# The first seven-product round's weight sums ahead of the low parts of x, and two of those low parts on GpSimd

## The reference

```python
def swiglu(x, w_gate, w_up, w_down):
    return (jax.nn.silu(x @ w_gate) * (x @ w_up)) @ w_down
f = swiglu(rms_norm_2(h, ffn1_pre_norm[l]), ffn1_w_gate[l], ffn1_w_up[l], ffn1_w_down[l])
h = h + FFN_RESIDUAL_WEIGHT * rms_norm_2(f, ffn1_post_norm[l])
```

## Time and profile before

| | us |
|---|---|
| median of three runs | 1831.26 |
| lowest, highest | 1829.66, 1832.38 |
| the profiled execution's own time | 1829.83 |
| its span in the trace | 1827.7 |
| TensorE busy | 1792.5 (98%) |
| GpSimd busy | 1286.9 (70%) |
| VectorE busy | 1126.0 (62%) |
| ScalarE busy | 710.5 (39%) |

### The profile page before, as it was taken

One profiled execution on the slowest core, in us unless ns is written; L12 is line 12 of the kernel. 1 busy time (PEld: TensorE's weight loads), 2 busy tenths in 40 slices (PEclk: granted clock), 3 DMA queues, 4 the chain that ended last, 5 costly groups with the idle time before them and its releaser, 6 DMA issues.

```text
span 1827.7 us, 28330 instructions
## 1 busy us (share of the span) xinstructions
PE 1792.5 (98%) x10236; PEld 1528.0 (84%) x10236; DVE 1126.0 (62%) x1741; ACT 710.5 (39%) x1337; POOL 1286.9 (70%) x1190
## 2 busy tenths in 40 slices
PE   9999999999999999999999999999999998999998
PEld 7888888878878899998888877798876778999886
DVE  5166774149984798887016767574454189888731
ACT  3111111127762366552014267553413255666001
POOL 7766666767777798877667865453772687888775
PEclk9999999999999999999999999999999999999999
DMA  5222223232223323235223311201321222323421
GB/s 187 94 91 92 92 92 138 92 120 78 89 69 116 131 100 103 106 109 189 95 92 104 103 60 47 69 26 47 116 95 44 93 110 76 115 96 113 165 101 69
DMA packets 25886, 179.36 MB, mean 98 GB/s; under 512 B 2864, under 2 KB 2992, under 8 KB 6704
## 3 DMA queue, kind: packets, MB, share of 16 engines
q1 hardware_dynamic: 24048, 168.31, 26.0%
q10 hardware_dynamic: 1728, 9.58, 1.4%
HBM read 171.58 MB, written 6.29 MB: 97 GB/s over the span
## 4 chain that ended last, share of the span: by engine, by line
PE 84%; DVE 8%; ACT 3%; issue 3%; POOL 1%; DMA 1%; DVEq 0%; ACTq 0%; POOLq 0%
PE bank L457 12%; PE bank L458 12%; PE bank L459 12%; PE bank L1216 6%; PE bank L1218 6%; PE bank L1217 6%; PE bank L1666 2%; PE bank L1667 2%; PE bank L1668 2%; PE bank L495 2%; PE bank L496 2%; PE bank L497 2%; DVE temps L1397 1%; PE bank L2071 1%; PE bank L2347 1%
## 5 line engine op out<-in xcount | busy, mean ns | idle before, releaser
L350 POOL TENSOR_TENSOR weights_lo<-raw_weights,weights_hi 128x512 fp32r<-128x512 f32 (+4 forms) x416 | 558.8, 1343 | 41.2 <-ACT weights_hi L369 7.4
L348 POOL TENSOR_SCALAR weights_hi<-raw_weights 128x512 fp32r<-128x512 f32 (+4 forms) x392 | 268.0, 684 | 340.1 <-PE bank L459 173.7
L457 PE MATMUL bank<-x_hi,weights_hi 128*128 128x512 f32 x688 | 271.5, 395 | 0.2
L459 PE MATMUL bank<-x_lo,weights_hi 128*128 128x512 f32 x688 | 267.9, 389 | 0.0
L458 PE MATMUL bank<-x_hi,weights_lo 128*128 128x512 f32 x688 | 267.8, 389 | 0.0
L457 PEld LDWEIGHTS bank<-x_hi,weights_hi 128*128 128x128 f32 x688 | 129.2, 188 | 28.1 <-POOL weights_lo L350 0.8
L459 PEld LDWEIGHTS bank<-x_lo,weights_hi 128*128 128x128 f32 x688 | 129.1, 188 | 27.1
L458 PEld LDWEIGHTS bank<-x_hi,weights_lo 128*128 128x128 f32 x688 | 129.2, 188 | 26.9 <-issue 1.0
L1218 PE MATMUL bank<-x_lo,weights_hi 128*128 128x256 f32 x432 | 122.2, 283 | 0.0
L1258 POOL TENSOR_TENSOR weights_lo<-temps,weights_hi 128x512 fp32r<-128x512 f32 x72 | 108.1, 1521 | 2.7 <-ACT weights_hi L1290 2.7
L1258 POOL TENSOR_TENSOR weights_lo<-raw_weights,weights_hi 128x512 fp32r<-128x512 f32 x72 | 97.6, 1360 | 13.3 <-ACT weights_hi L1290 13.0
(11 more groups left out here) (552 smaller groups left out, 5076.6 us busy)
## 6 DMA issues: line engine op xcount, KB each, us to landing
raw_weights<-in_ffn_seven SPq DMA_DIRECT2D x36, 1024.0 KB, 4.7
raw_weights<-in_a_ug SPq DMA_DIRECT2D x16, 1024.0 KB, 4.8
raw_weights<-in_b_in SPq DMA_DIRECT2D x12, 1024.0 KB, 4.8
raw_weights<-in_ffn_down SPq DMA_DIRECT2D x12, 1024.0 KB, 4.7
raw_weights<-in_ffn_down SPq DMA_DIRECT2D x7, 1408.0 KB, 6.2
raw_weights<-in_a_out SPq DMA_DIRECT2D x8, 1024.0 KB, 4.8
raw_weights<-in_ffn_up SPq DMA_DIRECT2D x8, 1024.0 KB, 4.8
raw_weights<-in_a_v SPq DMA_DIRECT2D x7, 1024.0 KB, 4.8
```

The lines of the kernel that those rows point to most:

```text
L348: nc.gpsimd.tensor_scalar(hi, raw, 1.0, 0.0, ALU.mult, ALU.add).then_inc(S("units_hi"), 1)
L350: nc.gpsimd.tensor_tensor(lo, raw, hi.bitcast(F32), ALU.subtract).then_inc(units_ready, 1)
L457: nc.tensor.matmul(ps, wh, xh[:, k, :], start=k == 0, stop=False)
L459: last = nc.tensor.matmul(ps, wh, xl[:, k, :], start=False, stop=k == last_k)
```

## The change

The four weight sums of round 0 and M5's low stand on VectorE behind plain round 1, ahead of the lows of x; the lows of x are then only numbers 0 and 1. Numbers 2 and 3 are made by GpSimd, behind its lows of M6 and M7 of round 0. So that the sums may lie in T[3] early, plain round 2 gates into T[1] instead of T[3], and ScalarE's copy of M5's half result (which also goes to T[1]) waits for that round's low. ScalarE makes the highs of M1, M5, M6, M3, M7 ahead of plain round 2's silu, M2's behind that round, and moves low 3 only behind M6's copy.

```diff
--- before.py
+++ after.py
@@ -169,7 +169,7 @@
     [("b_thr", KB), ("seven_hi", 2 * PRODUCTS * SEVEN)], [("b_a", KB), ("seven_kept", 2 * 3 * SEVEN)], [("b_scan", KB), ("seven_sums", 2 * 4 * SEVEN)],
     [("b_y", KB), ("seven_gates", 2 * SEVEN)], [("b_ix", KB), ("seven_joined", 2 * SEVEN)], [("b_bterm", KB), ("seven_lo_by_dve", 2 * SEVEN)],
     [("a_vn", KA), ("seven_lo", 2 * POOL_LOWS * SEVEN)], [("a_spatial", KA), ("seven_used", 2 * PRODUCTS * SEVEN)], [("b_tl", KB), ("kept_x", 5)],
-    *([(early, n)] + _members(kind, ("ffn1", each), ("ffn2", each)) for early, n, kind, each in (("b_a2", KB, "mixed_hi", 4), ("b_m2", KB, "mixed", 4), ("a_s_read", KA, "mixed_lo", 4), ("b_thi", KB, "moved", 2))),
+    *([(early, n)] + _members(kind, ("ffn1", each), ("ffn2", each)) for early, n, kind, each in (("b_a2", KB, "mixed_hi", 4), ("b_m2", KB, "mixed", 4), ("a_s_read", KA, "mixed_lo", 2), ("b_thi", KB, "moved", 2), ("a_gu", KA, "mixed_lo_by_pool", 2))),
     [("raw_first2", 16), ("spilled", 32)], [("raw_first3", 16), ("reloaded", 32)], [("x_in2", 16), ("raw_rest", 16)],
     [("b_mult", KB)] + _members("gained", ("ffn1", KD), ("ffn2", KD)),
     [("fx_o", FOXH), ("ma_o", 2 * MH)], [("fx_hi", FOXH // 2), ("ma_hi", 2 * MH)], [("fx_lo", FOXH // 2), ("ma_lo", 2 * MH)],
@@ -1225,10 +1225,10 @@
                     return lambda k: x[MIX_OF[p]][:, k, :]
 
                 def mixed_ready(t):
-                    if r == 0:
+                    if r == 0 and t < 2:
                         pe.wait_ge(*due(f"{f}_mixed_lo", t + 1))
-                        if t >= 2:
-                            pe.wait_ge(*due(f"{f}_moved", t - 1))
+                    elif r == 0:
+                        pe.wait_ge(*due(f"{f}_moved", t - 1))
 
                 pe_bank_read(pe, f, g, 1)
                 product(M1, up[:, A_HALF], plain(XH, 0, A_HALF), plain(XL, 0, A_HALF), True)
@@ -1248,6 +1248,10 @@
                 mixed_ready(3)
                 product(M4, up[:, A_HALF], mixed(MIX_H, M4), mixed(MIX_L, M4), False)
 
+        def pool_mixed_low(pool, f, t):
+            pool.wait_ge(*due(f"{f}_mixed_hi", t + 1))
+            nc.gpsimd.tensor_tensor(LOW_AT[t], MIX[t], MIX_H[t].bitcast(F32), ALU.subtract).then_inc(S(f"{f}_mixed_lo_by_pool"), 1)
+
         def pool_seven(pool, ph):
 
             for r in range(SEVEN):
@@ -1256,6 +1260,8 @@
                         continue
                     pool.wait_ge(*due("seven_hi", seven_count(ph, r, p)))
                     nc.gpsimd.tensor_tensor(RING_LO[p], source_of(r, p), RING_HI[p].bitcast(F32), ALU.subtract).then_inc(S("seven_lo"), 1)
+                    if r == 0 and p in (M6, M7):
+                        pool_mixed_low(pool, ph.name[:4], 2 if p == M6 else 3)
 
         def act_gained(act, f, src, gain, ready):
 
@@ -1273,7 +1279,7 @@
 
         def act_move_low(act, f, t):
             act.wait_ge(units_used, PH[f"{f}_up"].used(HEAD - 1, 3))
-            act.wait_ge(*due(f"{f}_mixed_lo", t + 1))
+            act.wait_ge(*due(f"{f}_mixed_lo_by_pool", t - 1))
             nc.scalar.activation(MIX_L[t], LOW_AT[t].bitcast(F32), ACT.Copy).then_inc(S(f"{f}_moved"), 1)
 
         def act_seven_hi(act, ph, r, p):
@@ -1305,16 +1311,16 @@
             ph = PH[f"{f}_seven"]
             for g in range(HEAD - 1):
                 if g == HEAD - 2:
-                    act_seven_hi(act, ph, 0, M1)
+                    for p in (M1, M5, M6, M3, M7):
+                        act_seven_hi(act, ph, 0, p)
                 act_silu(act, f, g, T[:, 0, :])
                 if f == "ffn2" and g == 0:
                     act_mixed_hi(act, f, 1)
                     act_mixed_hi(act, f, 2)
-                act_y_hi(act, f, g, T[:, 3, :])
+                act_y_hi(act, f, g, gated_tile(g))
                 if f == "ffn2" and g == 0:
                     act_mixed_hi(act, f, 3)
-            for p in range(M5, M4):
-                act_seven_hi(act, ph, 0, p)
+            act_seven_hi(act, ph, 0, M2)
             for r in range(SEVEN):
                 g, more = HEAD + r, r + 1 < SEVEN
                 gate, up = PS[2 * (r % 2)], PS[2 * (r % 2) + 1]
@@ -1324,14 +1330,17 @@
                 act_keep(act, ph, r, M1, KEPT[:, A_HALF], up[:, A_HALF])
                 if r == 0:
                     act_move_low(act, f, 2)
-                    act_move_low(act, f, 3)
                 if more:
                     act_seven_hi(act, ph, r + 1, M1)
+                if r == 0:
+                    act.wait_ge(*due(f"{f}_yl", HEAD - 1))
                 act_keep(act, ph, r, M5, KEPT5, gate[:, B_HALF])
                 if more:
                     act_seven_hi(act, ph, r + 1, M5)
                 act_y_hi(act, f, g - 1, old_up)
                 act_keep(act, ph, r, M6, KEPT[:, B_HALF], up[:, A_HALF])
+                if r == 0:
+                    act_move_low(act, f, 3)
                 if not more and f == "ffn1":
                     after_seven(act)
                 if more:
@@ -1346,6 +1355,10 @@
                 act_silu(act, f, g, T[:, 0, :])
                 act_y_hi(act, f, g, T[:, 3, :])
 
+        def gated_tile(g):
+
+            return T[:, 1 if g == HEAD - 2 else 3, :]
+
         def dve_ffn_plain(dve, f, ph, r, g, before_gated=None, before_low=None):
 
             bank = 2 * (g % 2)
@@ -1357,11 +1370,11 @@
                 before_gated()
             dve.wait_ge(*due(f"{f}_tu", g + 1))
             dve.wait_ge(*due(f"{f}_sg", g + 1))
-            nc.vector.tensor_tensor(T[:, 3, :], T[:, 1, :], T[:, 2, :], ALU.mult).then_inc(S(f"{f}_y"), 1)
+            nc.vector.tensor_tensor(gated_tile(g), T[:, 1, :], T[:, 2, :], ALU.mult).then_inc(S(f"{f}_y"), 1)
             if before_low:
                 before_low()
             dve.wait_ge(*due(f"{f}_yh", g + 1))
-            nc.vector.tensor_tensor(Y_L[:, g, :], T[:, 3, :], Y_H[:, g, :].bitcast(F32), ALU.subtract).then_inc(S(f"{f}_yl"), 1)
+            nc.vector.tensor_tensor(Y_L[:, g, :], gated_tile(g), Y_H[:, g, :].bitcast(F32), ALU.subtract).then_inc(S(f"{f}_yl"), 1)
 
         def dve_mix_x(dve, f, t):
 
@@ -1431,13 +1444,13 @@
             else:
                 dve_ffn_plain(dve, f, head, 0, 0)
             dve_ffn_plain(dve, f, head, 1, 1)
-            for t in range(4):
-                dve_mixed_low(dve, f, t)
-            dve_ffn_plain(dve, f, head, 2, 2)
-            dve.wait_ge(*due(f"{f}_yl", HEAD - 1))
+            dve.wait_ge(*due(f"{f}_yl", HEAD - 2))
             for p in (M5, M6, M3, M7):
                 dve_seven_sum(dve, ph, 0, p)
             dve_seven_low(dve, ph, 0)
+            for t in range(2):
+                dve_mixed_low(dve, f, t)
+            dve_ffn_plain(dve, f, head, 2, 2)
             last_head = HEAD - 1
             dve.wait_ge(units_used, head.used(last_head, 1))
             dve_gate_scaled(dve, f, PS[2 * (last_head % 2)])
```

## The result

The changed kernel has a median of 1833.6 us over 20 runs, the kernel before one of 1830.74 over 20 runs beside it: a ratio of 1.0015 with a 95% interval of 1.0008 to 1.0022. So it is slower, by 2.9 us, which is under the 0.2% that I had set as the bound of "no change" while the interval reaches over it. The span of the profiled execution went from 1827.7 to 1830.8 us.

A forecast was written before the change was run, and what follows sets the result against it. TensorE bounds the kernel, busy 1792.5 of 1827.7 us; M5's 3.3 us wait for VectorE's low was the longest. First FFN +3.1 and second +1.0 gave +4.1 on 1831.26, so 1835.4 us; range 1830.5 to 1838.0.

The forecast's parts named there:

- M1 waits in place of M5: Second FFN, first seven-product round: M1 waits for plain round 2's scalings to free its bank, starting 4.3 us late.
- A GpSimd low of x blocks for its whole length: VectorE beside GpSimd's 1024-wide lows: each low takes 2.4 us alone and holds VectorE up for all of it.
- The bound from a 512-wide block: Lower bound on VectorE's hold-up by a GpSimd low of x: 1.1 us, making the change's sum about zero (-0.2).
- The second FFN by round 3: Net delay of TensorE in the second FFN by round 3 of the seven-product rounds: +1.0 us.
- The first FFN: Gating and a sum fall behind GpSimd's wide lows, M4 in round 0 comes +2.9 us late; +3.1 by round 3.
- The turns of the later rounds: VectorE and GpSimd sharing time in the next two rounds: joins late by some tenths, as before.
- The total: Whole kernel: +3.1 in the first FFN and +1.0 in the second, together +4.1 us, so 1835.4.
- my likeliest class: Whole kernel's outcome: slower, chance 0.52, with the forecast just above the 0.2% (3.7 us) bound of no change.
- The named wait: Second FFN, before the change: M5's wait for its low on VectorE, with the slow clock behind it, costing about 4.8 us.
- the third rival: Both FFNs' pauses grow, a turn lost in each and the clock fallen in both: +6.9 us, 1838.2; chance 0.10.
- the simple replacement: M1 waits in M5's place, but wide GpSimd lows hold VectorE up little: -0.2 us, 1831.1; chance 0.22.
- The one in which GpSimd loses the turns: VectorE runs at its lone prices, M5's wait and slow clock go in the second FFN: -4.7 us, 1826.6; chance 0.10.

The follow-up runs named there:

- e3: The change with GpSimd's two wide lows shrunk to one column each, the low part of x in M7 and M4 not computed: 1827.74 us, ratio 0.9977 to before.
- v1: Kernel before with plain rounds 1 and 2 worked in banks and VectorE ordered by due dates, no low of x on GpSimd: 1827.0 us, ratio 0.9977.
- v2: Kernel before with VectorE ordered by due dates (M5's sum and low early), plain rounds not in banks: 1831.33 us, ratio 1.0003.
- e2: The change with the sums back behind plain round 2, two lows of x still on GpSimd: 1835.32 us, ratio 1.0019 to the kernel before.
- e1: The change's order on VectorE and ScalarE, but all four lows of x on VectorE: 1833.79 us, ratio 1.0010 to the kernel before.
- v0: Kernel before with plain rounds 1 and 2 scaled, gated and lowered in their banks, order and lows as before: 1828.63 us, ratio 0.9984.

## Why the prediction was right, and where it was off

It was right in the sign, in the mechanism and in round 0's places; that the two FFNs' sums came so near is in part luck. By its steps:

- *M1 waits in place of M5*: forecast +4.3 us in the second FFN; measured 4.08 of wait (4.24 with the restart). The scalings were forecast 14.6 us behind the start of VectorE's stretch; they ended at 1518.44, from 1503.92, 14.5.
- *A GpSimd low of x blocks for its whole length*: forecast VectorE instructions of 2.5 to 3 us beside it; measured 2.88 and 2.69. Its own price of 2.4: 2.38 where it met nothing. That the lock holds for the whole instruction, as the Trainium skill has it (page SBUF — State Buffer, the section on the two separate sides), the trace agrees with: 2.88 us for a low that takes 0.68 alone. The recorded lengths overlap a little, though: in turns a 512-wide step of each engine takes 1.7 us together, and 0.68 and 1.30 alone make 1.98. The bound from a 512-wide block, which would have made the change neutral, is refuted by these rows, and by e3.
- *The second FFN by round 3*: forecast +1.0, measured +0.9. M6 started at 1523.48, 1.7 later than before if M1's due times are laid together (forecast +1.8), and M4 0.6 later (forecast +0.7). But at M1 of round 2 nothing of this was left (-0.1), and the +0.9 is all round 2's new join wait. I had put the joins of the next two rounds down as "late by some tenths, as before". The agreement of the sum is luck.
- *The first FFN*: forecast +3.1, measured +2.6. This is the mis-sized term, and by more than the 0.5 shows: M4's delay in round 0 was forecast +2.9 and measured +1.7, and 1.0 of the 2.6 is again round 2's join, which was not forecast. For M4, I had the sum for M5 of round 1 fall behind the second wide low, and the sum got the turn: the rows have the two start at 644.94 and 644.93, and it took its lone 0.68. The later sum took the block, but the join came at 653.43 and not at 654.8. And I had added half of a clock fall behind a pause of 2.6 us; the pause was 1.69, and the granted clock from 653.8 to 657.1 is 1.00.
- *The turns of the later rounds*, put at nothing beyond before's tenths: 1.9 us. They don't come from a wide low, since e3, without them, has the same two waits; v1 and v2, with another order, have none in round 2.
- *The total*: forecast +4.1, measured +2.9. With two sums 0.6 too large, and 0.4 us of scatter in the rest of the program, it landed on the other side of the 0.2% from my likeliest class; 0.16 of the 0.38 for "same" was for that. (The spans moved by 3.1, the medians by 2.9.) Without round 2's unforeseen 1.9 us it would by this count have been about +1: round 0's loss was forecast at 3.6 (2.9 and 0.7) and measured at 2.1 (1.7 and 0.5).
- *Slips in the sums*: three rounds at 836 matmuls in 100 us are 30.1 us, not 30.2, so the second FFN lost 7.3 us and not 7.2, and the place can give back 9.4 and not 9.2. The named wait costs 3.4 + 1.3 = 4.7, not 4.8. The parts named for the +6.9 of the third rival add up to about 6.5. None of this moves the forecast.

Of the rivals, the simple replacement (-0.2) had the right picture of M1 but not of the first FFN. The one in which GpSimd loses the turns did not occur: in the rows read the two engines alternate, and where both came due within 0.2 us, VectorE was first twice (644.94, and 1544.76 before) and GpSimd once (1547.08). That the pause of 4 us lets the clock fall was forecast and seen; what it cost by itself was not tried; behind it M6 still waited 0.37 us for ScalarE, so not all of it can have counted.

What stays open is whether round 2's waits can be avoided in the change's order, and how the order would have done with GpSimd's lows put elsewhere in its queue; e2 shows only that behind M6 and M7 they delay M2.

## What to carry to other kernels

Before work is moved from VectorE to GpSimd, look at whether the instructions that stay on VectorE read two SBUF tiles: if so the two engines' times nearly add up, and the subtraction cost twice as much on GpSimd (2.38 us against 1.21), so that here the move gained nothing even where GpSimd was idle (e1 against the change). What does help is to make fewer such instructions: the same arithmetic with one operand in a bank ran at its lone price in every row read and was worth more than any order (v0, v1). And when a late product is cured by moving its work forward, ask what stands behind it in the same stream and when that is due: here it was the bank of the very next matmul.

## What the runs showed of the hardware that I had not expected

Splitting an instruction in two did not soften the contention: with two 512-wide lows in place of one of 1024 the time was the same (ratio 1.0014 against 1.0015), though the single waits moved by a microsecond.

The length of a pause of TensorE alone didn't tell whether the clock would fall: behind one of 2.16 us (v0) the granted clock was 0.61 for 3.2 us, behind one of 2.70 (e2, M2 in the second FFN) it was 1.00.

Which engine gets a turn was decided by 0.1 to 0.2 us and was worth 1.1 us, two rounds later too (1547.18 against 1544.76). Where two instructions came due within 0.1 us (644.94 and 644.93), I had the turn go the other way, and the join came 1.4 us earlier than I forecast (653.43 against 654.8): an estimate from rows is no finer than such turns.
